# Moving the streamed operands of a two-block network kernel by 64, 448 and 128 bytes against its weight buffers

## The reference, cut to what matters

```python
proj = jnp.einsum('btd,dc->btc', h, w_in[l])            # 2048 -> 8320 columns
y = jnp.einsum('btc,cd->btd', concat(o_rwkv, o_hgrn), w_out[l])
h = _layer_norm(ALPHA * h + y, ln_w[l], ln_b[l])
z = rms_norm(x, norm_g) @ w_in                          # latent layer: 3136 columns
q = rms_norm(cq, q_norm_g) @ w_q_up;  kv = rms_norm(ckv, kv_norm_g) @ w_kv_up
x = x + (o * jax.nn.silu(gate)) @ w_out                 # and again for the last layer, 8192 columns in
```

## The kernel before, in words

| buffer | before | after |
|---|---|---|
| `x_hi0`, `x_lo0`, `lat_hi`, `lat_lo` | 0 | 64 |
| `mla_q`, `mla_k`, `mla_sq` and the like, by way of the latents' arena | 0 | 64 |
| `x_hi1`, `x_lo1` | 0 | 448 |
| `o_hi4`, `o_lo4`, `mix`, `stage_start` | 0 | 128 |
| `mla_k_rope_hi` of the first and second head of a pair | 256, 320 | 384, 448 |
| `mla_k_rope_lo`, both heads | 128 | 256 |

## Time and profile before

### The profile page before, as it was taken

The page is one execution under the profiler, slowest core; times in us unless marked ns, Lnnn a source line. Parts: engine busy times, 40 slices in busy tenths (PEclk is TensorE's granted clock), DMA queues, the critical chain, the costliest instruction groups (busy, mean ns, idle before and its releaser), DMA issues.

```text
span 3081.9 us, 60223 instructions
## 1 busy us (share of the span) xinstructions
PE 3043.9 (99%) x19614; PEld 2482.4 (81%) x19614; DVE 1532.5 (50%) x2996; ACT 804.8 (26%) x1552; POOL 2074.1 (67%) x3468
## 2 busy tenths in 40 slices
PE   8999999999999999999999999999999999999999
PEld 7777777788888788788777778888888888888787
DVE  5566555567566766711566773154244324423600
ACT  2333333233232203200354552021112112211300
POOL 7555554578888696988733456897666766676675
PEclk9999999999999999999999999999999999999999
DMA  5222122132222232333211112332222322222142
GB/s 162 63 63 63 57 63 63 56 94 82 75 82 82 73 96 80 83 97 94 78 39 34 48 41 76 96 99 83 82 78 71 88 75 76 81 82 82 55 130 88
DMA packets 461253, 239.61 MB, mean 78 GB/s; under 512 B 27917, under 2 KB 456392, under 8 KB 461128
## 3 DMA queue, kind: packets, MB, share of 16 engines
q1 hardware_dynamic: 457148, 232.14, 25.9%
q10 hardware_dynamic: 3980, 5.63, 0.5%
HBM read 233.52 MB, written 4.19 MB: 77 GB/s over the span
## 4 chain that ended last, share of the span: by engine, by line
PE 91%; DVE 5%; issue 2%; ACT 1%; DMA 0%; POOL 0%; DVEq 0%; ACTq 0%; SPq 0%; PEldq 0%; POOLq 0%
PE proj L349 25%; PE proj L351 24%; PE proj L350 24%; PE work L2614 2%; PE work L2196 2%; PE work L2189 1%; PE work L349 1%; PE work L351 1%; PE work L350 1%; PE work L730 1%; PE work L744 1%; PE work L1308 1%; PE work L1547 1%; PE work L1561 1%; DVE lat_sq L1851 0%
## 5 line engine op out<-in xcount | busy, mean ns | idle before, releaser
L321 POOL TENSOR_SCALAR w_hi<-raw_weights 128x256 fp32r<-128x256 f32 x1728 | 788.6, 465 | 974.6 <-DMA raw_weights<-w_in 337.3
L325 POOL TENSOR_TENSOR w_lo<-raw_weights,w_hi 128x256 fp32r<-128x256 f32 x1728 | 1345.9, 789 | 0.0
L349 PE MATMUL proj<-x_hi,w_hi 128*128 128x512 f32 x2976 | 1204.1, 405 | 6.1 <-DVE x_lo L1839 4.2
L351 PE MATMUL proj<-x_hi,w_lo 128*128 128x512 f32 x2976 | 1163.7, 391 | 0.0
L350 PE MATMUL proj<-x_lo,w_hi 128*128 128x512 f32 x2976 | 1161.1, 390 | 0.0
L349 PEld LDWEIGHTS proj<-x_hi,w_hi 128*128 128x128 f32 x2976 | 560.0, 188 | 136.4 <-POOL w_lo L325 12.4
L351 PEld LDWEIGHTS proj<-x_hi,w_lo 128*128 128x128 f32 x2976 | 559.2, 188 | 121.2
L350 PEld LDWEIGHTS proj<-x_lo,w_hi 128*128 128x128 f32 x2976 | 560.9, 188 | 105.8 <-issue 2.2
L349 PE MATMUL proj<-o_hi,w_hi 128*128 128x512 f32 x253 | 100.3, 397 | 0.5 <-POOL w_lo L325 0.4
L350 PE MATMUL proj<-o_lo,w_hi 128*128 128x512 f32 x253 | 98.8, 390 | 0.0
L351 PE MATMUL proj<-o_hi,w_lo 128*128 128x512 f32 x253 | 98.7, 390 | 0.0
(11 more groups left out here) (497 smaller groups left out, 3934.0 us busy)
## 6 DMA issues: line engine op xcount, KB each, us to landing
raw_weights<-w_in SPq DMA_DIRECT2D x260, 256.0 KB, 3.1
raw_weights<-b_w_in SPq DMA_DIRECT2D x256, 256.0 KB, 3.1
raw_weights<-a_w_in SPq DMA_DIRECT2D x100, 256.0 KB, 3.2
raw_weights<-w_out SPq DMA_DIRECT2D x64, 256.0 KB, 2.9
raw_weights<-a_w_out SPq DMA_DIRECT2D x64, 256.0 KB, 2.9
raw_weights<-b_w_out SPq DMA_DIRECT2D x64, 256.0 KB, 2.9
raw_weights<-a_w_kv_up SPq DMA_DIRECT2D x32, 256.0 KB, 2.7
mix<-x SPq DMA_DIRECT2D x4, 1024.0 KB, 8.7
```

The source lines that it names most:

```text
L321: pool.tensor_scalar(part(hi_v, s, q), part(raw_v, s, q), 1.0, 1.0, ALU.mult, ALU.mult).then_inc(hi_done, 1)
L325: pool.tensor_tensor(part(lo_v, s, q - 1), part(raw_v, s, q - 1), part(hi_v, s, q - 1).bitcast(F32), ALU.subtract).then_inc(w_split, 1)
L349: pe.matmul(out, w_h, a_h, start=start, stop=False)
L351: return pe.matmul(out, w_l, a_h, start=False, stop=stop)
```

## The change

Three paddings are put in place of one: `lead(n)` moves the arena to the next address that lies n bytes, modulo 512, behind the weights. No instruction is added, removed or moved to another place in an engine's sequence; only addresses differ. The four weight slots stay where they were, as do the constants ahead of them. Everything from `x_start` on moves up, by 64 bytes for group 0, 448 for group 1 and 640 for `mix` and all behind it.

```diff
@@ -236,9 +236,14 @@
         n_small = fixed.take("n_small", 72)
-        fixed.at += (weights_at - fixed.at) % 512
+        lead = lambda n: (weights_at + n - fixed.at) % 512
+        fixed.at += lead(64)
         x_start = fixed.at
-        x_parts = [[fixed.take(f"x_{part}{g}", UNIT_KB * SEQ, F32R) for part in ("hi", "lo")] for g in range(2)]
+        x_parts = []
+        for g in range(2):
+            fixed.at += lead((64, 448)[g])
+            x_parts.append([fixed.take(f"x_{part}{g}", UNIT_KB * SEQ, F32R) for part in ("hi", "lo")])
+        fixed.at += lead(128)
         o_start = fixed.at
         mix = fixed.take("mix", KB * SEQ)
         stage_start = fixed.at
```

## The result

The changed kernel takes 3114.54 us (median of 3 runs, 3114.32 to 3115.34) against 3082.94 us: ratio 1.010, 95% interval 1.0081 to 1.012. So it is about 1% slower, by 31.6 us. The forecast was 3115 us.

The account below looks back on a forecast made before the run. TensorE was taken as the bound, through the distance between 512-column streams. From 3083.75 us, 28 us for x and latents and 4 us for outputs' parts gave 3115.75, predicted as 3115 us; range for 8 in 10: 3056 to 3142.

Parts of the forecast that it names:

- What bounds the kernel: Whole kernel: TensorE, busy 3043.9 of 3081.9 us, sets the end by the distance between starts of 10,359 streams of 512 columns.
- The sum: Groups 0 and 1 and latents 9600 streams x 2.9 ns = 28 us, outputs' parts 759 x 5 = 4 us.
- The relation between the addresses matters: Attention's rope streams: offset 256 beside the weights costs nothing, 128 costs 6 ns, so a stream's relative address affects its time.
- Cost repeats every 256 bytes: Stream offsets from the weights: 0 and 256 cost the same, so 64 would equal 320 and 448 equal 192.
- 64 is like 320 and is dear: Group 0 and latents at 64: priced like rope stream 320 (398 ns record), taken as 393.5 against 390.6, 2.9 ns a stream.
- Neither group is settled: Groups 0 and 1 of x stay at the unsettled stages' level, 393.5 ns, so switching offsets between them costs nothing more.
- Lengths can serve for distances: Matmul records: some ns longer means a next start as much later, 389 with 226.7 and near 395 with 232.5.
- each group settles again: Rival for groups of x: settled 226.7 ns returns, only 372 switches cost, 4 to 11 us; 3093 us, chance 0.12.
- Nothing changes: Rival for all streams: every matmul meets all address relations whatever its start; 3083 us, 3079 to 3088, chance 0.20.
- Faster, because 0 is a bad meeting point: Rival for all streams: reads collide most at equal offset, gain 17 to 37 us; put at 3064 us, chance 0.34.
- What would show it: Signs: out projection median 392 or more, starts 229 ns or more apart, means on x 393 to 394, o_lo about 395.

Follow-up runs that it names:

- all_up: All buffers, weights too, 64 bytes higher than in the kernel before, every distance between them kept: 3084.55 us, ratio 1.0005.
- all256: Kernel before with both groups of x, the latents and the outputs' parts at offset 256 from the weights: 3082.24 us.
- g0_only: Kernel before with only group 0 of x and the latents at offset 64, group 1 and outputs' parts at 0: 3096.11 us, ratio 1.0045.
- s224_0: Kernel before with group 0 of x and the latents at offset 224, all else at 0: 3125.5 us.
- before: The kernel without the change, streams at offset 0 from the weights: median 3083.05 us over 20 runs.
- s96_160: Kernel before with group 0 of x and the latents at offset 96, group 1 at 160, outputs' parts at 0: 3133.46 us.

## Why the prediction was right

- *What bounds the kernel: right.* Clock, chain, waits and weight loads stand still, and the span follows the distance between streams.
- *The sum: right, 32 us forecast, 31.6 measured.* Its terms, over the distances counted above: `x` 2.9 ns a stream forecast (26 us), 3.4 measured, but for 8,086 distances and not 8,928, since the rest follow a smaller matmul (28 us); latents 2.9 forecast, 1.1 measured (0.5 us in place of 2); outputs' parts 5 forecast, 5.0 measured (4 us); attention left out, 0.7 us measured. TensorE's idle time, put at no change, fell by 2 us. The misses cancel.
- *"The relation between the addresses matters": right, and shown by `all_up`,* which moves all and changes nothing. That the two reads get in each other's way is an explanation of it that no run tests.
- *"Cost repeats every 256 bytes": right,* shown by `all256`, by 320 with 64, and by 192 with 448.
- *"64 is like 320 and is dear": half right.* It is like 320, but it is the cheapest offset after 0, 2.2 ns. The 398 of the earlier trace rows was the first moment of a change, not a settled price. The dear one is 448, that is 192, which no row had shown: 6.7 ns.
- *"Neither group is settled": wrong.* This step failed. I gave both groups the level of the unsettled stages, and what happened is that each settles at a level of its own. The average comes out near it: the levels are 4.4 ns above 226.67 over all streams, and the excess over the levels falls from 1.3 to 0.3 ns, which leaves the 3.4 ns measured. That the two effects make nearly my 2.9 is luck. By stage the mean rose by 1.1 ns in the recurrence (150 to 550 us), which was at 230.4 before, by 3.0 from 600 to 1080 us, by 3.7 from 2100 to 2850, by 4.3 to 4.6 in the other long even stretches, and by 5 in the first output projection with what lies around it.
- *"Lengths can serve for distances": wrong between different states.* At 64 L355 has records of 388 ns and starts 228.9 apart, at 0 389 and 226.7.
- *The rival "each group settles again"* named the right kind of state and the right order for a switch, and failed in its premise that a settled state is always 226.7 ns. Its price was uncertain too: a change there and back costs 0.07 us in `g0_only`, against 0.02 to 0.06 forecast, and nothing that can be seen in the changed kernel. Its lower bound of 3088 us leaves out the outputs' 4 us; with them it is 3091.
- *"Nothing changes"* fell: eight offsets, all else alike, give 226.7 to 234.3 ns. From the rule of the Trainium skill ("TensorE: Matmul & The Clock Gate", section "Step-by-step: what each phase is for"), two independent read ports for stream and weights, the prediction drew a sum of 0, and that isn't borne out by this kernel.
- *"Faster, because 0 is a bad meeting point"* fell: of eight offsets modulo 256, 0 is the best. The 216 ns that the Trainium skill (same page, section "Back-to-back issue gap") gives for a single matmul taken by itself are the mean of no run.
- *What would show it.* A median of L355 of 392 or more in the output projection was asked for, and it is 393. Means on `x` of 393 to 394 were asked for, and they are 395 and 394; for `o_lo` about 395, and it is 394; starts 229 ns apart or more, and they are 228.9 and 233.3. Two signs moved unasked. POOL went from 2074.1 to 2083.8 us, and lies between 2067.9 and 2082.5 in the other kernels. DVE went from 1532.5 to 1507.7 us; that is less than the span moved and of the other sign, and in the other kernels it lies between 1521 and 1546 without a relation to their time. Of these 24.8 us, L967 (L962 before) has 5.4, L1654 (L1649) 4.4 and L2803 (L2798) 3.7; the rest is open. DVE was off the path in all kernels but `s224_0`, so its sum says nothing of the span.

## What to carry to other kernels

Where TensorE is busy all the time and streams 512 columns with a new weight block each, place the stream's buffers at a multiple of 256 bytes from the weight buffers, all of them alike: here other offsets for the groups cost 0.4 to 1.7%. Read the pace from starts, first and last over a counted window; a line's record length can fall while the pace gets worse. And a state seen just after an interruption isn't the state that an endless stretch goes to: price a steady stretch from a steady stretch, and if there is none, give the range both ends.

## What the runs showed of the hardware that was not expected

- With streams and weights at a fixed offset TensorE falls into a constant distance or a repeating cycle of two to seven matmuls, and its mean depends on the offset modulo 256 (the table above): 226.67 ns at 0, 228.9 at 64, 232.4 to 234.3 elsewhere. At 128 two such states were seen, 232.4 and 233.3.
- At the lower clock level streams start 426 or 427 ns apart, 512 clocks, at offset 0 (`before`) and at 96 or 160 (`s96_160`) alike.
- A triple with one operand at 64 and two at 0 (232.0 ns) is slower than with all at 64 (228.9).
- Half a weight block beside the same streams is slower (229.8 ns) than a whole one (226.7).
- A DVE addition with both inputs in SBUF took 29 us in place of 0.7 while POOL worked without a gap (`s224_0`); it cost TensorE 11 us and then ten distances of 427 ns in place of 227.
